# Branches two and three of the mixer merge: seven half-size products for four outputs, sums on VectorE, three gatings in four on GpSimd

## The reference, cut to what matters

```python
proj = h @ w_in
...
g = jax.nn.sigmoid(gates).reshape(b, s, N_BRANCH, D_MODEL)
merged = g[:, :, 0] * (y_fox @ w_branch[0]) + g[:, :, 1] * (y_ml @ w_branch[1]) + g[:, :, 2] * (y_hg @ w_branch[2])
return merged @ w_out
```

## Time and profile before

| | us |
|---|---|
| median of 3 runs | 2461.05 (2460.74 to 2464.88) |
| the profiled execution | 2473.3 |
| its span | 2471.6 |
| TensorE busy | 2399.9 (97%) |
| VectorE busy | 1177.4 (48%) |
| ScalarE busy | 483.1 (20%) |
| GpSimd busy | 616.1 (25%) |
| L1313, the branch stage on TensorE, 384 records | 165.0 |

### The profile page before, as it was taken

One profiled execution on the slowest core, in us unless ns is written; L12 is line 12 of the kernel. 1 busy time (PEld: TensorE's weight loads), 2 busy tenths in 40 slices (PEclk: granted clock), 3 DMA queues, 4 the chain that ended last, 5 costly groups with the idle time before them and its releaser, 6 DMA issues.

```text
span 2471.6 us, 32897 instructions
## 1 busy us (share of the span) xinstructions
PE 2399.9 (97%) x8544; PEld 1171.5 (47%) x8545; DVE 1177.4 (48%) x2744; ACT 483.1 (20%) x892; POOL 616.1 (25%) x628
## 2 busy tenths in 40 slices
PE   5999999999999999999999999999999999999997
PEld 3444444555544555566444554444444444444443
DVE  3376222666655576666244667433333333343332
ACT  3311000444432133333211112200000000000000
POOL 0000000000022100000211244555445545455541
PEclk9999999999999999999999999999999999999998
DMA  8231334343373233212334314489899999999995
GB/s 260 49 71 46 81 72 123 116 122 105 124 192 68 60 81 98 94 55 78 129 115 135 99 52 177 164 287 315 274 300 324 326 320 330 303 358 360 326 319 136
DMA packets 121190, 435.26 MB, mean 176 GB/s; under 512 B 21004, under 2 KB 23260, under 8 KB 95376
## 3 DMA queue, kind: packets, MB, share of 16 engines
q1 hardware_dynamic: 78208, 306.91, 35.7%
q0 software_dynamic: 42896, 127.25, 19.3%
HBM read 366.44 MB, written 71.70 MB: 177 GB/s over the span
## 4 chain that ended last, share of the span: by engine, by line
PE 86%; DVE 7%; another core or an unknown queue 2%; issue 1%; DMA 1%; ACT 1%; SPq 1%; POOL 0%; DVEq 0%; ACTq 0%; POOLq 0%
PE psum L980 22%; PE psum L1464 17%; PE psum L1531 8%; PE psum L1065 8%; PE psum L1313 7%; PE psum L1469 3%; PE psum L1330 3%; PE psum L1270 2%; PE psum L1537 2%; PE psum L1374 2%; PE psum L1136 2%; PE psum L1146 2%; PE psum L1155 2%; PE psum L1397 1%
## 5 line engine op out<-in xcount | busy, mean ns | idle before, releaser
L980 PE MATMUL psum<-mem 128*128 128x512 f32 x1536 | 690.1, 594 | 1.1 <-DMA mem<-in_w_in 0.9
L1464 PE MATMUL psum<-mem 128*128 x1008 | 449.9, 594 | 1.6 <-DVE mem L2678 1.0
L980 PEld LDWEIGHTS psum<-mem 128*128 128x128 f32 x1536 | 279.2, 191 | 293.9 <-issue 290.5
L785 POOL DMA_INDIRECT mem<-h_d,idx x287 | 293.7, 1023 | 368.9 <-DVE idx L2779 270.4
L1464 PEld LDWEIGHTS psum<-mem 128*128 128x128 f32 x1008 | 186.4, 190 | 229.9 <-issue 229.9
L2757 DVE TENSOR_TENSOR mem<-mem,psum 128x256 f32<-128x256 f32 x93 | 39.1, 421 | 438.0 <-ACT mem L1943 391.9
L1531 PE MATMUL psum<-mem 128*128 128x512 f32 x504 | 229.7, 603 | 10.0 <-ACT mem L1946 9.8
L1065 PE MATMUL psum<-mem 128*128 128x512 f32 x448 | 192.8, 592 | 0.0
L790 POOL DMA_INDIRECT out_x<-mem,put x93 | 140.5, 1511 | 98.9 <-issue 72.6
L1313 PE MATMUL psum<-mem 128*128 128x512 f32 x384 | 165.0, 592 | 0.0
L1531 PEld LDWEIGHTS psum<-mem 128*128 128x128 f32 x504 | 93.4, 191 | 135.0 <-issue 135.0
(11 more groups left out here) (424 smaller groups left out, 2478.0 us busy)
## 6 DMA issues: line engine op xcount, KB each, us to landing
mem<-in_exp_w SPq DMA_DIRECT2D x201, 1024.0 KB
mem<-in_w_in SPq DMA_DIRECT2D x16, 2048.0 KB, 14.3
proj_d<-mem SPq DMA_DIRECT2D x104, 256.0 KB, 2.0
mem<-in_ada_w POOLq DMA_DIRECT2D x16, 1024.0 KB, 6.2
mem<-proj_d POOLq DMA_DIRECT2D x56, 256.0 KB, 2.9
mem<-proj_d POOLq DMA_DIRECT2D x20, 512.0 KB, 5.6
mem<-in_ada_w SPq DMA_DIRECT2D x4, 2048.0 KB, 23.2
mem<-in_w_branch SPq DMA_DIRECT2D x3, 2048.0 KB, 8.0
```

The source lines that it names most:

```text
L785: g.indirect_dma_start(x[:, 2 * P * n:2 * P * (n + 1)], None, h2_q, bass.IndirectOffsetOnAxis(ap=idx[:, p, j, n:n + 1], axis=0), bounds_ch ...
L980: mm = t.matmul(bank(unit_bank(u)), l, r, start=(k == 0), stop=(k == KD - 1))
L1464: return t.matmul(bank(up_banks[j][r]), xgT[r][:, k, P * j:P * (j + 1)], up_piece(h, r, k), start=(k == 0), stop=(k == KD - 1))
```

## The change

Branch one stays as it was, 16 plain units. Branches two and three become 8 groups, four per branch. A group c of a branch covers the output blocks j = c and j = c + 4 and both token halves: four outputs, made by seven products of two matmuls (half of the 512 channels each). The banks x, y, z, u are 3, 2, 1, 0 in even groups and 7, 6, 5, 4 in odd ones.

- *Forms.* Per branch VectorE makes 8 sums of 1024 columns (`branch_form`), some in place in the weights and in the activations. Those of branch two stand behind every second plain unit. Of branch three the first four stand in groups 0 to 3, and the last four at the head of group 4, behind a wait for all of branch two's products.
- *Products.* TensorE makes x, z, x again (added), y, u, z again, u again. Product 3 waits for ScalarE's copy of x, product 6 for VectorE's first q3, product 7 for its second.
- *Sums.* ScalarE copies the first product (`q1s`). VectorE makes q2 = q1 + y, q3 = q2 + z, then q3 + u, q4 = q2 + z, q2 + u.
- *Gating.* Output 4n is multiplied by its gate on VectorE out of PSUM, the other three by GpSimd, in SBUF, in the gate's buffer. All four are added to `hT` by VectorE (`merge`), the last three of a group in the next group.
- *Gates.* There are six buffers `gt` and not three. GpSimd issues four loads behind each group's three multiplies.
- *scale_out* runs in groups 4 to 7, four in each, between the first and the second q3 add.
- *The end.* TensorE waits for 29 of the 32 sums ahead of the output projection and for 31 ahead of its eighth matmul. The slots are released at the same places of the loop as before: after the plain units, after group 3, after group 7.

The core of the diff. The new semaphore names are old ones counted on (s_q1 counts ScalarE's copies, s_qa VectorE's four sums of a group, s_fm the forms, s_gp GpSimd's products).

```diff
-        gt = [view(12288 + 512 * j, BW) for j in range(3)]
-        prod = [view(13824 + 512 * j, BW) for j in range(2)]
+        gt = [view(at, BW) for at in (12288, 12800, 13312, 0, 512, 1024)]
+        q1s, q2s, q3s, q4s = (view(at, BW) for at in (13824, 14336, 14848, 1536))
+        half_form = lambda at: view(at, 2, BW)
+        yf = {1: dict(zip((2, 3, 4), map(half_form, (18432, 19456, 20480)))), 2: dict(zip((2, 3, 4), map(half_form, (4096, 2048, 6144))))}
+        bf = {1: dict(zip((2, 3, 4), map(half_form, (21504, 24256, 26624)))), 2: dict(zip((2, 3, 4), map(half_form, (5120, 3072, 7168))))}
...
+        PLAIN, GROUPS = 16, 8
+        gate_place = lambda t: (1 + t // 16, t // 4 % 4 + 4 * (t % 4 in (1, 2)), t % 4 % 2)
+        gate_slot = lambda t: (1, 2, 0, 3, 4, 5)[t % 6]
+        gate_loads = lambda t: t // 6 + 1 + (5, 5, 6, 2, 2, 1)[t % 6]
+        gate_row = lambda br, j, half: row_of[f"g{br * 2 + j // 4}"] + (j % 4) * 2 + half
+        added_order = [0]
+        for g_ in range(1, GROUPS):
+            added_order += [4 * g_ - 3, 4 * g_ - 2, 4 * g_, 4 * g_ - 1]
+        added_order += [4 * GROUPS - 3, 4 * GROUPS - 2, 4 * GROUPS - 1]
+        merged = {t: n + 1 for n, t in enumerate(added_order)}
+        group_banks = lambda g: (3, 2, 1, 0) if g % 2 == 0 else (7, 6, 5, 4)
+
+        def branch_weights(br):
+            w = flat(slot(("wb", br))).rearrange("p (k n) -> p k n", k=4)
+            return [w[:, 2 * k:2 * k + 2, BW * i:BW * (i + 1)] for i, k in product(range(2), range(2))]
+
+        def branch_rows(br):
+            return [yT[br][:, 2 * k:2 * k + 2, BW * h:BW * (h + 1)] for k, h in product(range(2), range(2))]

...
+            def load_gate(t):
+                row = gate_row(*gate_place(t))
+                rows_stored(pool, row, 1)
+                g.dma_start(gt[gate_slot(t)], proj_d[row]).then_inc(s_g[gate_slot(t)], 16)
...
+            for t_ in range(3):
+                pool.wait_ge(s_pr, PLAIN - 2 + t_)
+                load_gate(t_)
+            pool.wait_ge(s_br, PLAIN)
+            for t_ in range(3, 6):
+                load_gate(t_)
+            for n in range(GROUPS):
+                for i, made in ((1, q3s), (2, q4s), (3, q2s)):
+                    t_ = 4 * n + i
+                    pool.wait_ge(s_qa, QA0 + 4 * n + 1 + i)
+                    pool.wait_ge(s_gs, PLAIN + t_ + 1)
+                    x = gt[gate_slot(t_)]
+                    g.tensor_tensor(x, x, made, ALU.mult).then_inc(s_gp, 1)
+                for t_ in range(4 * n + 6, min(4 * n + 10, 4 * GROUPS)):
+                    pool.wait_ge(s_mg, merged[t_ - 6])
+                    load_gate(t_)
...
+            def branch_product(to, l, r, first=True):
+                for k in range(2):
+                    mm = t.matmul(bank(to), l[:, k, :], r[:, k, :], start=first and k == 0, stop=(k == 1), skip_group_check=not first)
+                mm.then_inc(s_br, 1)
+
+            for n in range(GROUPS):
+                br, c = 1 + n // 4, n % 4
+                cut = lambda v: v[:, :, P * c:P * (c + 1)]
+                a11, a12, a21, a22 = map(cut, branch_weights(br))
+                b11, b12, b21, b22 = branch_rows(br)
+                x, y, z, u = group_banks(n)
+                forms = 8 * (br - 1)
+                if c == 0:
+                    block_ready(pe, ("wb", br))
+                if n == 1:
+                    pe.wait_ge(h_yc, HH)
+                if n >= 2:
+                    pe.wait_ge(s_qa, QA0 + 4 * (n - 1))
+                branch_product(x, a11, b11)
+                pe.wait_ge(s_fm, FM0 + forms + 2)
+                if n == 0:
+                    pe.wait_ge(s_pr, PLAIN - 2)
+                branch_product(z, cut(bf[br][3]), yf[br][3])
+                pe.wait_ge(s_q1, Q10 + n + 1)
+                branch_product(x, a12, b21, first=False)
+                pe.wait_ge(s_fm, FM0 + forms + 6)
+                if n == 0:
+                    pe.wait_ge(s_pr, PLAIN - 1)
+                branch_product(y, cut(bf[br][2]), yf[br][2])
+                if n == 0:
+                    pe.wait_ge(s_pr, PLAIN)
+                branch_product(u, a21, b12)
+                pe.wait_ge(s_fm, FM0 + forms + 7)
+                pe.wait_ge(s_qa, QA0 + 4 * n + 1)
+                branch_product(z, a22, yf[br][4], first=False)
+                pe.wait_ge(s_fm, FM0 + forms + 8)
+                pe.wait_ge(s_qa, QA0 + 4 * n + 2)
+                branch_product(u, cut(bf[br][4]), b22, first=False)
+
+            pe.wait_ge(s_mg, 29)

...
+                    if i == 0 and half == 0 and k == KD - 1:
+                        pe.wait_ge(s_mg, 31)
...
+            def gate(t):
+                act.wait_ge(s_g[gate_slot(t)], 16 * gate_loads(t))
+                x = gt[gate_slot(t)]
+                s.activation(x, x, ACT.Sigmoid).then_inc(s_gs, 1)
+
+            gate(0)
+            gate(1)
+            for n in range(GROUPS):
+                act.wait_ge(s_br, PLAIN + 7 * n + 1)
+                if n >= 1:
+                    act.wait_ge(s_qa, QA0 + 4 * n - 3)
+                s.activation(q1s, bank(group_banks(n)[0]), ACT.Copy).then_inc(s_q1, 1)
+                for t_ in range(4 * n + 2, min(4 * n + 6, 4 * GROUPS)):
+                    gate(t_)
...
+            def branch_form(br, n):
+
+                a11, a12, a21, a22 = branch_weights(br)
+                b11, b12, b21, b22 = branch_rows(br)
+                if n == 0:
+                    if br == 1:
+                        dve.wait_ge(m_yc, NT)
+                    else:
+                        dve.wait_ge(h_yc, HH)
+                    block_ready(dve, ("wb", br))
+                    ins = v.tensor_tensor(yf[br][3], b22, b12, ALU.subtract)
+                elif n == 1:
+                    ins = v.tensor_tensor(bf[br][3], a11, a21, ALU.subtract)
+                elif n == 2:
+                    ins = v.tensor_tensor(b12, b12, b11, ALU.subtract)
+                elif n == 3:
+                    ins = v.tensor_tensor(a21, a21, a22, ALU.add)
+                elif n == 4:
+                    dve.wait_ge(s_fm, FM0 + 8 * (br - 1) + 4)
+                    ins = v.tensor_tensor(yf[br][2], b22, b12, ALU.subtract)
+                elif n == 5:
+                    ins = v.tensor_tensor(bf[br][2], a21, a11, ALU.subtract)
+                elif n == 6:
+                    dve.wait_ge(s_fm, FM0 + 8 * (br - 1) + 6)
+                    ins = v.tensor_tensor(yf[br][4], b21, yf[br][2], ALU.subtract)
+                else:
+                    ins = v.tensor_tensor(bf[br][4], a12, bf[br][2], ALU.subtract)
+                ins.then_inc(s_fm, 1)
+
+            def merge(t):
+
+                if t % 4:
+                    dve.wait_ge(s_gp, GP0 + 3 * (t // 4) + t % 4)
+                _, j, half = gate_place(t)
                 dst = hT[:, j, half * BW:(half + 1) * BW]
+                v.tensor_tensor(dst, dst, gt[gate_slot(t)], ALU.add).then_inc(s_mg, 1)
+
+            for n in range(PLAIN):
+                dst = hT[:, n // 2, n % 2 * BW:(n % 2 + 1) * BW]
                 dve.wait_ge(s_gs, n + 1)
                 dve.wait_ge(s_br, n + 1)
-                if br == 0:
-                    v.tensor_tensor(dst, gt[n % 3], bank(n % 3), ALU.mult).then_inc(s_pr, 1)
+                v.tensor_tensor(dst, gt[n % 3], bank(n % 3), ALU.mult).then_inc(s_pr, 1)
+                if n % 2 == 1:
+                    branch_form(1, n // 2)
+            dve.wait_ge(s_pr, PLAIN)
+            for n in range(GROUPS):
+                x, y, z, u = group_banks(n)
+                made = PLAIN + 7 * n
+                if n >= 4:
+                    dve.wait_ge(s_mg, merged[4 * (n - 4) + 3])
+                if n == 4:
+                    dve.wait_ge(s_br, PLAIN + 28)
+                    for m in range(4, 8):
+                        branch_form(2, m)
+                if n >= 1:
+                    merge(4 * n - 3)
+                    merge(4 * n - 2)
+                dve.wait_ge(s_gs, PLAIN + 4 * n + 1)
+                dve.wait_ge(s_br, made + 3)
+                own = gt[gate_slot(4 * n)]
+                link(v.tensor_tensor(own, own, bank(x), ALU.mult))
+                merge(4 * n)
+                if n >= 1:
+                    merge(4 * n - 1)
+                dve.wait_ge(s_q1, Q10 + n + 1)
+                dve.wait_ge(s_br, made + 4)
+                link(v.tensor_tensor(q2s, q1s, bank(y), ALU.add))
+                v.tensor_tensor(q3s, q2s, bank(z), ALU.add).then_inc(s_qa, 1)
+                if n < 4:
+                    branch_form(2, n)
                 else:
-                    v.tensor_tensor(prod[n % 2], gt[n % 3], bank(n % 3), ALU.mult).then_inc(s_pr, 1)
-                    dve.wait_ge(s_pr, n + 1)
-                    v.tensor_tensor(dst, dst, prod[n % 2], ALU.add).then_inc(s_mg, 1)
-                if 26 <= n < 34:
-                    scale_out(0, n - 26)
-                if 40 <= n < 48:
-                    scale_out(1, n - 40)
+                    for m in range(4):
```

(51 more changed lines are left out.)

## The result

The kernel after takes 2494.51 us (median of 5 runs, 2490.86 to 2500.95) against 2460.74 (2460.26 to 2464.88) before on the same chip: ratio 1.0143, interval 1.0132 to 1.0154. That is 34 us slower, where 2 us faster was forecast. Its profiled execution took 2500.95, span 2499.2.

What follows compares the result with a forecast made beforehand. TensorE was taken to bound the stage, without idle; 16 fewer matmuls save 13.73 us, and stalls, lock and late x take back all but 2.2, giving 2458.9 us against the median 2461.05, range 2453 to 2465.

Steps and rivals of the forecast that it cites:

- the shift passes on whole: After the output projection, a serial chain then the experts: the stage's change carries through unchanged to the total time.
- 24 multiplies, hidden: GpSimd's products, three a group at 1.26 us each: with load issues 5.9 of 12 us, done in time, hidden.
- the rivals: Saving survives (2453.5 us, 27%), GpSimd and VectorE block each other (2467.7, 12%), x comes late (2461, 9%).
- the sum: All forecast terms together, 13.73 us saved against stalls, lock and late x: -2.2 us.
- Groups 1 to 3: Branch stage: product 6 stalls 0.32 us and product 7 0.03, 0.35 per group, 1.05 for three.
- Group 4 up to product 6: Four last branch-three forms go first on VectorE, delaying product 6 by 1.68 us, plus 1.26 for the lock.
- the prediction's lock: GpSimd's multiplies hold up VectorE's SBUF work by up to 1.26 us each; priced only in group 4, 1.26.
- Groups 5 to 7: Product 6 stalls 0.32 us, product 7 1.33 behind four scale_out multiplies: 1.65 per group, 4.95 for three.
- Group 4 behind product 6: In group 4, scale_out multiplies before the second q3 add stall product 7 by 1.33 us.
- The end: First x tile, asked for later behind list and g2b, delays the first residual by 1.2 us, bounds 0 and 3.3.
- Rival 2, GpSimd against VectorE: Branch stage: one GpSimd multiply a group blocks VectorE before product 6, 10.1 us replacing 1.26; 2467.7 us, 12%.

Runs made afterwards that it cites:

- the loop at 597: The changed kernel as recorded, its experts loop starting at instruction 597 of GpSimd's program instead of before's 551: 2494.51 us against 2460.74, ratio 1.0143.
- the same edit at 679: Changed kernel plus 82 idle GpSimd instructions, so the experts loop starts at instruction 679: 2477.22 us against 2476.77 of before, ratio 1.0008.
- the reordered kernel: Changed kernel, loop at 679, scale_outs moved, branch-three forms spread, older add later, list sent in group 4, g2b after two x tiles: 2461.60 us against 2472.92, ratio 0.9950.
- at 638: Reordered stage with 40 added GpSimd instructions, experts loop starting at instruction 638: 2450.97 us against 2459.94 of before, ratio 0.9967.
- the moved multiplies: Changed kernel, loop at 679, scale_outs of groups 4 to 7 moved behind the second q3 and q4 adds: 2471.34 us against 2472.92 of before, ratio 0.9997.

## Why the prediction was wrong

The step that failed is the last one: "What follows is a serial chain, then the experts [...] the shift passes on whole." It took the loop over the experts as untouched, because none of its lines were edited. Its price was 0; it measured +1.43% in the whole time with the loop at 597, against +0.08% for the same edit at 679. The prediction counted GpSimd's added instructions as busy time (24 multiplies, hidden, which was right) and not as length of its program. None of the rivals had it either. Of the 35.6 us by which 2494.51 misses the forecast of 2458.9, the place makes some 33 (1.0143 against 1.0008); up to the first residual the trace is within 1 us of the sum. The page of before could not show it: 37 packets of q14 are no sign of how near 597 is.

The steps within the stage, from the distances between the first matmuls of products:

- *Groups 1 to 3.* Forecast 12.01 + 0.35 = 12.36 a group; 1286.88 - 1274.45 = 12.43. Right.
- *Group 4 up to product 6.* Forecast 12.01 + 0.03 + 1.68 + 1.26 = 14.98; 1301.62 - 1286.88 = 14.74. Right, with the form that a multiply of GpSimd holds up (the prediction's lock) 1.07 longer instead of 1.26 (below).
- *Groups 5 to 7.* Forecast 12.01 + 1.65 = 13.66; 1329.84 - 1316.14 = 13.70. The idle before product 7 is named as expected, VectorE's L2604 (1.05 us; from product 6 to product 7 it is 1319.14 - 1316.14 = 3.00 instead of 1.716, so 1.28 against the 1.33 forecast). Moving the `scale_out` took it away.
- *Group 4 behind product 6.* Forecast 13.66; 1316.14 - 1301.62 = 14.52, 0.86 more. The windows below show the cause, which I had not priced: behind the long wait the granted clock was down (0.72 in 1304 to 1308 us).
- *The end.* Forecast: x late by 1.2 us. The residual began 1363.68 - 1348.34 = 15.34 us after the output projection, and 14.11 before: 1.2 late. The 1.2 was chosen between bounds of 0 and 3.3, so that it is met so closely is partly luck. It is dearer as soon as the stage is shorter (3.1).
- *Rival 2, GpSimd against VectorE.* Not what made it slower. That the two hold each other up, the prediction's lock, is there. VectorE's timeline at 1291 us, and below it GpSimd's:

```profile
1291.21 1.22 DVE L2548 TENSOR_TENSOR mem<-mem 128x1024 f32<-128x1024 f32 x1
1292.35 2.29 DVE L2550 TENSOR_TENSOR mem<-mem 128x1024 f32<-128x1024 f32 x1
...
1291.37 2.18 POOL L779 TENSOR_TENSOR mem<-mem 128x512 f32<-128x512 f32 x1 [0.32 <-DVE mem L2608]
```

The form that met a multiply took 2.29 and not 1.22, 1.07 more; the multiply itself took 2.18 and not 1.26. It started 0.16 us behind the form before, which took its usual 1.22. In the usual group the two merges meet one in slack: at 1321.74 us they took 2.36 instead of 1.29, and VectorE then idled 2.26 us until TensorE's next product was ready. The 30 us that 24 meetings on the path would have made, at 1.26 each, did not come.

- *Does the stage's gain pass on?* From stage start to residual the reordered kernel is 11.7 us shorter than before and by its ratios gains 12 (interval 9 to 16) or, at 638, 8 (5 to 11). For after at 679 and for the moved multiplies the same sum is 0.5 and 5.3 us (1363.20 - 1184.95 and 1360.32 - 1186.90, against 178.75), and the ratios give -2 (-4.5 to 0.2) and 0.7 (-1.5 to 3.0). Some 2 to 5 us are missing there. With the multiplies moved, 1.7 us of them lie behind the residual: because x was late, TensorE idled 4.49 us ahead of the transposes (1.40 before), the granted clock was 0.62 in 1368 to 1372 us, and the eight transposes and the next 8 matmuls took 1.48 and 8.16 us instead of 1.09 and 6.87. In after the same place idled 2.63 us and took 1.97 and 7.35, 1.4 us more. So the late x cost more than its own lateness, which the prediction did not price. In after with its loop at 679 the idle was 3.65 us and nothing was lost there. Where the rest goes is open.

## What to carry to other kernels

Before pricing an edit, count the instructions that it adds to each engine ahead of a run-time loop: the same loop made the kernel 0.6 to 2.1% slower at some places of GpSimd's program. Read the instruction queues' packets (205 against 37 here) and the share of "issue" in the chain (12% against 1%) first whenever a kernel changes far from its edit, and repeat it with idle instructions added, at more than one place, before judging the edit: here 46 led from a good place to a bad one, and 40 back to a good one. A wait behind a stage takes back some of what the stage saves once it is the later one (with the multiplies moved, x put the residual 17.20 us behind the start of the output projection instead of 14.11), so move it together with the stage.

## What the runs showed of the hardware that was not expected

The packets of an instruction queue depend on where a loop lies: 6 packets of 8 KB within the loop over the experts or 175, with the same loop of 342 instructions. One of GpSimd's waits ended by "issue" lasted up to 7.58 us (ahead of the gather at 2207.28 us in after), beside DMA engines at a share of 0.87 to 0.95.

One idle of 2.47 us can be followed by a lower clock of TensorE. Windows after, 1300 to 1316 us (us, busy us and instructions by engine, granted clock, DMA share, GB/s):

```profile
1300.00:1304.00 4.00, 2.38 (x4) 0.68 (x4) 3.97 (x8) 1.79 (x3) 0.54 (x1) 0.86 0.51 144
1304.00:1308.00 4.00, 3.53 (x7) 1.60 (x7) 1.65 (x3) 0.10 (x1) 2.49 (x2) 0.72 0.00 0
1308.00:1312.00 4.00, 4.00 (x11) 1.75 (x10) 2.40 (x3) 0.60 (x1) 3.24 (x4) 1.00 0.22 62
```

The mean is 0.72 in 1304 to 1308, and one matmul record between 1301 and 1317 us took 1191 ns instead of 592. In the kernel with the `scale_out` moved the idle before product 6 of group 4 was the same 2.47, and there the group that followed took its usual 12.26. In after with its loop at 679 the clock was down again (0.63 in 1300 to 1304). So after an idle of this length the clock was sometimes lower and sometimes not; what decides is open. With two forms fewer ahead of it in the reordered kernel the idle is gone, and the mean granted clock is 1.00 through all groups.
